# Bank read-outs as a condition for the attention steps of the second block

## The reference, cut to what matters

```
for l in range(2):                      # second block
    hx, hc = modulate(rms_norm(x)), modulate(rms_norm(ctx))     # factors from adaln(c), adaln(c_ctx)
    if l == 0: y_x, y_c = even_mixer(hx, hc)   # 4 heads softmax - lam * softmax, 4 heads latent attention
    else:      y_x      = odd_mixer(hx, hc)    # 16 heads, local part with a bias table, context part without
    x = x + g_a * (y_x @ w_out);   x = x + g_f * swiglu(modulate(rms_norm(x)))
    if l == 0: the same for ctx
```

## Time and profile before

| | before |
|---|---|
| median of 3 runs | 2504.06 us (2503.77 to 2506.32) |
| profiled execution | 2508.06 us, span 2506.3 us, mean granted clock 0.997 |
| TensorE matmul busy | 2458.2 us, 98% |
| TensorE weight load | 2146.4 us, 86% |
| VectorE busy | 1664.4 us, 66% |
| ScalarE busy | 1284.1 us, 51% |
| POOL busy | 225.2 us, 9% |
| context's attention | about 1444 to 1541 us |
| x's attention, even layer | about 1697 to 1813 us |
| odd attention | about 2184 to 2283 us |

### The profile page before, as it was taken

The page is one execution under the profiler, slowest core; times in us unless marked ns, Lnnn a source line. Parts: engine busy times, 40 slices in busy tenths (PEclk is TensorE's granted clock), DMA queues, the critical chain, the costliest instruction groups (busy, mean ns, idle before and its releaser), DMA issues.

```text
span 2506.3 us, 40594 instructions
## 1 busy us (share of the span) xinstructions
PE 2458.2 (98%) x16401; PEld 2146.4 (86%) x16401; DVE 1664.4 (66%) x2448; ACT 1284.1 (51%) x1854; POOL 225.2 (9%) x306
## 2 busy tenths in 40 slices
PE   8999999999999999999999999999999999999999
PEld 8998877889989988877888988888889898756998
DVE  5556786875566566776776668776666656776555
ACT  4444645454444446454554555655555445565443
POOL 1000000111002000000111201220000101211000
PEclk9999999999999999999999999999999999999999
DMA  8755565758658655556666646663456657735564
GB/s 284 242 181 175 145 188 157 282 173 294 206 176 273 188 158 165 168 162 233 223 212 189 192 135 207 197 209 120 135 181 196 196 184 202 220 123 164 186 185 143
DMA packets 239370, 479.14 MB, mean 191 GB/s; under 512 B 17584, under 2 KB 38328, under 8 KB 239120
## 3 DMA queue, kind: packets, MB, share of 16 engines
q1 hardware_dynamic: 215664, 397.07, 50.4%
q0 software_dynamic: 23520, 79.49, 9.7%
HBM read 475.33 MB, written 6.92 MB: 192 GB/s over the span
## 4 chain that ended last, share of the span: by engine, by line
PE 84%; DVE 9%; ACT 3%; issue 2%; DMA 2%; POOL 0%; SPq 0%; ACTq 0%; DVEq 0%; POOLq 0%
PE bank L213 81%; PE bank L216 3%; DVE wlo L156 2%; ACT whi L200 1%; DMA raw<-in_od_w_in 1%; DVE bank L161 1%; DVE xl L156 0%; ACT bank L200 0%; DVE dssc L185 0%; ACT sps L200 0%; DVE dssc L164 0%; DMA raw<-in_ffn_w_out 0%; DVE zs L156 0%; DVE st L176 0%; DVE sg L156 0%
## 5 line engine op out<-in xcount | busy, mean ns | idle before, releaser
L156 DVE TENSOR_TENSOR wlo<-raw,whi 128x1024 fp32r<-128x1024 f32 (+3 forms) x786 | 915.4, 1171 | 633.4 <-ACT whi L200 631.9
L200 ACT ACTIVATE whi<-raw 128x1024 fp32r<-128x1024 f32 (+3 forms) x786 | 794.3, 1018 | 704.1 <-PE bank L213 650.9
L213 PE MATMUL bank<-xh,whi 128*128 128x256 f32 x2208 | 626.8, 284 | 3.4 <-DVE xl L156 2.4
L213 PE MATMUL bank<-xl,whi 128*128 128x256 f32 x2208 | 621.0, 281 | 0.0
L213 PE MATMUL bank<-xh,wlo 128*128 128x256 f32 x2208 | 620.8, 281 | 0.0
L213 PEld LDWEIGHTS bank<-xh,whi 128*128 128x128 f32 x2208 | 417.8, 189 | 15.1 <-issue 7.5
L213 PEld LDWEIGHTS bank<-xl,whi 128*128 128x128 f32 x2208 | 417.9, 189 | 0.6
L213 PEld LDWEIGHTS bank<-xh,wlo 128*128 128x128 f32 x2208 | 417.8, 189 | 0.0
L213 PE MATMUL bank<-whi,xh 128*128 128x512 f32 (+2 forms) x632 | 253.7, 401 | 7.4 <-DVE xl L156 3.9
L213 PE MATMUL bank<-wlo,xh 128*128 128x512 f32 (+2 forms) x632 | 246.1, 389 | 0.0
L213 PE MATMUL bank<-whi,xl 128*128 128x512 f32 (+2 forms) x632 | 245.8, 389 | 0.0
(11 more groups left out here) (452 smaller groups left out, 3761.4 us busy)
## 6 DMA issues: line engine op xcount, KB each, us to landing
raw<-in_ffn_w_in SPq DMA_DIRECT2D x280, 512.0 KB, 4.4
raw<-in_ffn_w_out SPq DMA_DIRECT2D x154, 512.0 KB, 4.5
raw<-in_w_mix_in SPq DMA_DIRECT2D x112, 512.0 KB, 3.6
store<-in_mod_w POOLq DMA_DIRECT2D x46, 512.0 KB, 8.0
raw<-in_od_w_in SPq DMA_DIRECT2D x40, 512.0 KB, 4.8
stow<-in_mod_w POOLq DMA_DIRECT2D x30, 512.0 KB, 4.7
raw<-in_ffn_w_in SPq DMA_DIRECT2D x56, 256.0 KB, 2.8
raw<-in_w_branch SPq DMA_DIRECT2D x24, 512.0 KB, 3.3
```

Source lines behind the costliest of these rows:

```text
L156: return self.passed(out, self.e and self.e.tensor_tensor(out, a, b, op))
L200: return self.made(us, self.e and self.e.activation(out, a, f, **k))
L213: return self.made(n, self.e and self.e.matmul(out, lhs, rhs, **k))
```

## The change

A function `coming(co, n)` gives the `drained` marks of the n banks that `next_bank` would give next, as things stand when it is called. The two attentions add these marks to the need that ends a step: three banks in `Even.attend`, four in `Odd.attend`. The step that follows is thus resumed only when these banks are reckoned read out, besides what it needed before. Nothing else is changed.

```diff
+def coming(co, n):
+
+    free = sorted((b for b in co.banks if not b.held), key=lambda b: b.since)
+    return [b.drained for b in free[:n]]
@@ Even.attend
-            yield Need(st.get(i - 2), st.get(i - 1))
+            yield Need(st.get(i - 2), st.get(i - 1), coming(co, 3))
@@ Odd.attend
-            yield Need(st.get(i - 4), st.get(i - 2))
+            yield Need(st.get(i - 4), st.get(i - 2), coming(co, 4))
```

## The result

The changed kernel takes 2517.48 us, median of four runs (2515.72 to 2518.07), against 2504.44 us for the kernel before, also over four (2503.77 to 2506.32). The ratio is 1.0049, 95% interval 1.0037 to 1.0061: 13.0 us slower, where I had forecast 2507.2 and a range up to 2511.8. A later repetition on another occasion gave 2515.28 against 2504.6 us, 1.0045 (1.0032 to 1.0057), 10.7 us. I take the places from the traces and the totals from the medians.

The account below looks back on a forecast made before the run. TensorE was taken as nearly always busy, except a 4.84 us odd-attention stall plus 2.7 us of clock. Terms -1.8 + 4.1 - 1.5 + 2.0 + 0.3 = +3.1 us on 2504.06: 2507.2 us; range 2498.8 to 2511.8.

Parts of the forecast that it names:

- Wherever a block already stands between two steps I expect nothing: Even attentions: one weight block outlasts reduction, negation and Exp, so no cost there; term +0.3 us, ends 0 and +2.
- the context's attention uncovered: Rival, context's attention: three feed-forward blocks spent earlier leave three steps bare at 1.5 us each; +7.6, 2511.7 us, chance 0.23.
- The stall's term: Odd attention, step 4: two modulation groups and a block fill the 4.84 us wait for `rtg`; -1.8 us, clock loss unchanged.
- at about 2202.8, 0.7 us before the scores can start: Odd attention's stall: when the value block that goes ahead can start, its bank drained; counted as 0.7 us gained.
- Taking them out saves nothing: The two late gaps, ended by VectorE: removing their five and three modulation groups gains no time.
- The far end of the term, -6.7: Odd attention's stall, best case: clock kept as well and the block's time filled, -6.7 us.
- clock kept: Rival, odd attention's stall: filled so that the clock stays up; gain 6.7, cost 1.5, so -5.2, 2498.9 us, chance 0.15.
- The tiles suffice: Odd attention from 2233: five modulation tiles, each landed 4.7 us after issue, cover more than two groups per 3.7 us step.
- So at least two groups go into each step: Odd attention's stretch with steps alone: two modulation groups per step instead of one, 9 more at 0.45 us, +4.1 us.
- At most 1.5 us come back: After the odd attention: four groups drawn from 2267 on free TensorE until the next block, which needs `xl`; -1.5 us.
- A bare gap should lower it too: +2.0: First late gap, before 2292: grown to 3.7 us without groups, it lowers the clock; +2.0 us, ends 0 and +2.7.
- The second gap: nothing: Second late gap, before 2309: already long, so losing its three groups changes nothing.

Follow-up runs that it names:

- the best kernel: The whole change without its condition in the context's even attention, the last 8 of 96 modulation groups kept for the gaps after the odd attention: 2500.89 us, 0.9986 of before.
- the kernel with the late steps alone: Kernel before plus the condition only in the odd attention, for steps from 8 on, four banks: 2513.96 us, 1.0037 of before.
- odd only with 8 kept: Kernel before plus the condition in the odd attention alone, the last 8 modulation groups kept for the gaps after it: 2506.42 us, 1.0006 of before.
- the late steps with 8 groups kept: Kernel before plus the condition for odd-attention steps from 8 on, the last 8 modulation groups kept for the gaps: 2509.07 us, 1.0015 of before.

## Why the prediction was wrong

**"Wherever a block already stands between two steps I expect nothing" failed.** It was sized at 0.3 us, with 2 as its upper end. The context's attention alone costs 4.8 us, of which its trace shows 3.1 at the transposes of `yc`; behind them it first wins 1.9 back and then has three groups and 0.9 us of waits for tiles left over behind `y`. I had priced what the waiting step does, and looked for the uncovered steps inside the attention. What counts is the last block of the feed-forward, which covered the norm that comes after the attention. The rival "the context's attention uncovered" had the right place and a wrong threshold: not "from the third block taken" but from the first, and the price is one wait for a norm with its clock, not three steps of 1.5 us. Its sum, 2511.7, was the nearest of all, and still 5.8 us short. The earlier trace rows holds the hint: one block between two steps, the last of its stream, so that a block drawn forward is missing at the end.

Taken out of the whole change, the same condition is worth 7.9 us (10.7 to 2.8, between two occasions), more than its own 4.8. With it the odd attention waits 3.7 us for tiles, without it for none, and 20 groups instead of 18 stand between 1500 and the first odd scores. The condition shifts all that is reckoned after it, so the parts aren't a sum: 4.8 and 6.7 and 2.7 make 14.2, and the whole is 10.7 to 13.0.

**The stall's term, -1.8 us, named a gain that doesn't exist.** With the condition at step 4 alone the order came out as forecast (two groups, then a block, before step 4), and the gain was 0. The step that failed is "at about 2202.8, 0.7 us before the scores can start": I reckoned the filled time as won, though VectorE was busy for 4.43 of 4.50 us, as I had myself read in the earlier trace rows, and 2.30 us of wait came back at the next transposes. And I counted 1.14 us for two groups that come out of gaps of which the same prediction says "Taking them out saves nothing". The term also takes the condition to act at step 4 only. It puts back steps 1 to 3 as well, and the stall goes, wholly and with its clock, where these are spaced by two blocks: in the whole change, which loses the gain again to tiles and their clock, and in the best kernel, which keeps it. The far end of the term, -6.7, and the size of the rival "clock kept" were thus near the truth, through another mechanism: the earlier steps put back, not the waiting one.

**"The tiles suffice" failed.** I used the 4.7 us of the earlier trace rows for refills that would be issued in a bunch. Seven `stow` refills in that stretch took 6.6 us in the middle, while all DMA engines were busy (share 1.01 to 1.03, 389 to 416 GB/s), and TensorE waited 3.7 us, during and after which the clock was at 0.93 and 0.63. The planner reckons a tile of 1024 columns landed 3 + 0.0016 x 1024 = 4.6 us after its issue, sooner than it was here, so nothing in the order guarded against it. By the Trainium skill, page "DMA: Bandwidth & Descriptors", section "Anatomy of one DMA — SWDGE (gpsimd) path", a DMA of GpSimd costs about 2.0 us and its bytes at 436 GB/s, an estimate of 3.2 us for 512 KB alone; no run here has such a transfer alone. The same page, section "Specifications", gives 435 GB/s as the ceiling of the fabric, which the 416 of the window nearly reaches, and about 358 GB/s as the limit of one core's share of HBM, which the windows' 389 to 416 exceed, so that here the measurement decides. What the trace shows is that refills which take 4.7 us in mixed traffic take 6.6 to 7.0 when bunched. That the full DMA engines are the cause is argued from the share of 1.01 to 1.03 beside it, and no run changed the traffic alone.

**What held.** "So at least two groups go into each step": 9 more were forecast, at +4.1 us; it was 12 more, and +5.2 us in the kernel with the late steps alone. The first gap grew to 3.65 us, as forecast ("from 1.36 to 3.7"), and the clock behind it fell to 0.66. The instruction count differs by 4, as said.

**The terms behind the stretch came out by luck.** "At most 1.5 us come back" was 0: the removed groups became 1.95 us of waiting for `xl`, since `xl` ends the wait wherever the groups stand. "A bare gap should lower it too: +2.0" was +1.4 to +1.5, and in the repetition of the same program 0. "The second gap: nothing" was -1.0, because groups also put `modb` on VectorE, the engine that ends that gap. -1.5 + 2.0 = +0.5 was forecast, +0.3 measured in the late steps' kernel and -0.1 in the whole, out of three terms that were each off by 0.5 to 1.5 us.

**What stays open.** The trace of after shows some 9 us up to the transposes of `y`, the medians 10.7 to 13.0; the condition for the late steps shows 5.3 of 9.0. Single executions of one kernel differ by 2 us and more, and each kernel but the whole change has a single trace, so I can't place the rest. Nor is it settled what x's condition alone costs (0 to 4.5 us). Yet in company it helps: odd only with 8 kept is +1.2, with x's condition added -3.7. The idle time of the stretch is 4.2 us in the one and 1.9 in the other. The traces show one difference ahead of it: with x's condition 20 groups stand between 1500 and the first odd scores, without it 17, so the stretch has three fewer to take (11 and 14) and waits 0.3 us for tiles instead of 3.0. Whether those three groups are the cause was not tested by itself.

## What to carry to other kernels

A condition in a planner removes no wait; it moves work forward, and the price is what it leaves bare at the end of the stream it draws from: look first at the last block of each stream and at the gaps that the filler covers now. Filler that gaps will need later should be reserved for them, and its refills need a margin for landing in company, not alone. Parts of such a change don't add up, so test them apart and together: here the whole cost 10.7 to 13.0 us, and the same condition in two of three places with 8 groups kept won 3.7.

## What the runs showed of the hardware

Nine refills and one weight load of 512 KB within 16 us kept the DMA engines' share at 1.01 to 1.03 and moved 389 to 416 GB/s; the refills landed in 6.6 and 7.0 us instead of 4.7, the load in 8.8 instead of 3.3.

The granted clock behind a short gap is not given by the gap. Behind 3.65 us it was 0.66 in the profile of after. In the repetition, the same program, it was 1.00 behind the same gap:

```profile
2299.42 0.47 PE L213 MATMUL bank<-whi,xh 128*128 128x512 f32 x1 [3.66 <-DVE xl L156]
```

```profile
2300.00:2304.00 4.00, 4.00 (x19) 3.22 (x18) 1.36 (x2) 1.06 (x1) 0.00 (x0) 1.00 0.40 115
```

The transposes of `yc`, behind 2.93 us, took 3.46 us in the one and 2.38 in the other, and 1.97 at full clock with the context's condition alone. Behind 1.95 us the clock stayed at 1.00 in eight traces and fell in four; this is one of the four, the late steps with 8 groups kept:

```profile
2271.70:2276.30 4.60, 4.56 (x14) 3.16 (x16) 2.38 (x4) 1.12 (x2) 0.00 (x0) 0.63 0.18 55
```

Behind 1.36 us it stayed in all ten traces that have this gap; behind 3.65 us it fell in eight of nine. So a gap of 2 to 4 us costs 0 or 1.3 to 2.8 us of clock in these traces; that this is one source of the 2 us by which single executions differ is likely, but only one program has two traces. The Trainium skill, page "TensorE: Matmul & The Clock Gate", Part 1, says that the point of the change varies from run to run because the hardware's observation doesn't start with the kernel. The two traces of one program agree with it. I had put such a loss into the sum as a sure +2.0; it is a chance.
